# Twelve head-norm statistics, each as two single-pass matmuls on high and low parts, at later places in the matrix queue

## The reference

```python
    S_new, o = retention_scan(qf, kf, vf, ret_state.astype(jnp.float32))   # 4 heads, 256 values each
    o = o * lax.rsqrt(jnp.mean(o * o, axis=-1, keepdims=True) + EPS)       # the head norm
    o = o.reshape(B, T, RET_V_WIDTH).astype(xn.dtype)
    b_out = (jax.nn.silu(g) * o) @ w_ret_out
    merged = jax.nn.sigmoid(gate_a) * a_out + jax.nn.sigmoid(gate_b) * b_out
    return merged @ w_o, new_buf, S_new
```

## Time and profile before

| what | value |
|---|---|
| median of 3 runs (range) | 1497.55 us (1497.22 to 1497.59) |
| the profiled execution's span | 1495.6 us |
| outside the span, median less span | 1.95 us |
| PE busy | 1475.2 us (99%) |
| PE on the chain that ended last | 96% of the span |
| DVE, ACT, POOL busy | 1001.0, 635.4, 842.0 us |
| mean granted clock of PE | 0.997 |
| the 24 rows of L1194 (12 statistics) | 8.9 us of PE busy |

### The profile page before, as it was taken

The page is one execution under the profiler, slowest core; times in us unless marked ns, Lnnn a source line. Parts: engine busy times, 40 slices in busy tenths (PEclk is TensorE's granted clock), DMA queues, the critical chain, the costliest instruction groups (busy, mean ns, idle before and its releaser), DMA issues.

```text
span 1495.6 us, 28307 instructions
## 1 busy us (share of the span) xinstructions
PE 1475.2 (99%) x11336; PEld 1455.2 (97%) x11336; DVE 1001.0 (67%) x1251; ACT 635.4 (42%) x929; POOL 842.0 (56%) x571
## 2 busy tenths in 40 slices
PE   8999999999999999999999999999999999999996
PEld 5999999999999999999999999999999999999995
DVE  7999888856545724576715876766657765574847
ACT  5533444344544541131213855556556332332333
POOL 3377776777545653257565445555555655554555
PEclk9999999999999999999999999999999999999998
DMA  6013333322356258621421144566759575454634
GB/s 217 22 42 94 114 114 113 113 80 65 112 176 205 75 200 296 219 80 50 149 78 50 29 149 171 199 237 219 253 193 326 203 285 189 142 208 156 227 107 170
DMA packets 110091, 229.13 MB, mean 153 GB/s; under 512 B 8960, under 2 KB 20992, under 8 KB 108304
## 3 DMA queue, kind: packets, MB, share of 16 engines
q1 hardware_dynamic: 95296, 204.30, 39.7%
q10 hardware_dynamic: 14672, 23.09, 4.6%
HBM read 154.41 MB, written 72.95 MB: 152 GB/s over the span
## 4 chain that ended last, share of the span: by engine, by line
PE 96%; POOL 1%; DMA 1%; ACT 1%; issue 1%; DVE 0%; POOLq 0%; SPq 0%; DVEq 0%; ACTq 0%
PE ps L1476 40%; PE ps L1237 26%; PE ps L1026 16%; PE ps L1402 3%; PE ps L1389 3%; PE ps L1074 2%; PE ps L1164 1%; PE ps L1169 1%; PE ps L1180 1%; PE ps L1166 1%; DMA cva_h<-conv_scratch 1%; PE ps L1147 0%; PE ps L1152 0%; PE ps L1194 0%; POOL w_l L931 0%
## 5 line engine op out<-in xcount | busy, mean ns | idle before, releaser
L1476 PE MATMUL ps<-tx_h,w_h 128*128 128x258 f32 x960 | 271.5, 283 | 0.0
L1476 PE MATMUL ps<-tx_l,w_h 128*128 128x258 f32 x960 | 271.3, 283 | 0.0
L1476 PE MATMUL ps<-tx_h,w_l 128*128 128x258 f32 x960 | 271.1, 282 | 0.0
L996 POOL TENSOR_TENSOR w_l<-raw,w_h 128x512 fp32r<-128x512 f32 x120 | 185.6, 1551 | 147.6 <-ACT w_h L2033 147.1
L1476 PE MATMUL ps<-fx_l,w_h 128*128 128x258 f32 x720 | 203.7, 283 | 0.0
L1476 PE MATMUL ps<-fx_h,w_h 128*128 128x258 f32 x720 | 203.6, 283 | 0.0
L1476 PE MATMUL ps<-fx_h,w_l 128*128 128x258 f32 x720 | 203.4, 282 | 0.0
L1476 PEld LDWEIGHTS ps<-tx_h,w_h 128*128 128x128 f32 x960 | 181.4, 189 | 0.1
L1476 PEld LDWEIGHTS ps<-tx_l,w_h 128*128 128x128 f32 x960 | 181.4, 189 | 0.1
L1476 PEld LDWEIGHTS ps<-tx_h,w_l 128*128 128x128 f32 x960 | 181.2, 189 | 0.0
L2328 DVE SCALAR_TENSOR_TENSOR ps<-u_ext,wdw,ps 128x512 f32<-128x512 f32 x232 | 155.2, 749 | 0.0
(11 more groups left out here) (386 smaller groups left out, 4305.4 us busy)
## 6 DMA issues: line engine op xcount, KB each, us to landing
raw<-wseq_dram SPq DMA_DIRECT2D x260, 256.0 KB, 3.1
quad_scratch<-quad_h SPq DMA_DIRECT2D x16, 774.0 KB, 3.5
tx_h<-quad_scratch SPq DMA_DIRECT2D x12, 1032.0 KB, 10.4
tx_l<-hidden_scratch SPq DMA_DIRECT2D x12, 1032.0 KB, 12.8
gate_scratch<-gst SPq DMA_DIRECT2D x10, 1032.0 KB, 5.0
hidden_scratch<-hq_g SPq DMA_DIRECT2D x8, 1032.0 KB, 7.0
hidden_scratch<-stg_b SPq DMA_DIRECT2D x6, 1032.0 KB, 6.9
hq_g<-hidden_scratch SPq DMA_DIRECT2D x6, 1032.0 KB, 13.1
```

What stands on the lines that cost most here:

```text
L996: pool.tensor_tensor(lo, src, hi.bitcast(F32), ALU.subtract).then_inc(q_lo, 1)
L1476: out = pe.matmul(ps[:, 2 * n + s, 0:HC], RINGS[q % RING][wa][:, kk * P:(kk + 1) * P], OPS[x][xb][:, QK * kh + kk, at_:at_ + HC], start=(i ...
```

## The change

Each statistic is computed by two single-pass matmuls in place of one plain float32 matmul. To feed them, ACT copies the summed squares into a high part (`square_hi`), and DVE subtracts it to get the low part (`square_lo`). High and low parts have buffers of their own, so in the second pair a square no longer waits for the statistic two before it, but for that one's low part. The statistics stand later in PE's queue: one turn later in the first pair for i = 0, 1, 2, 4 and 5 and two for i = 3, and one or two slots later in the second. In the second pair squares, sums, roots and the decode store are reordered around them. Two semaphores are merged into others at the start of the kernel (`x0_sq` into `x_sq`, `hist_ld` into `wdw_ld`).

```diff
-NORM_SQUARE = {20: 0, 24: 1, 28: 2, 32: 3, 39: 4, 42: 5}
+NORM_SQUARE = {20: 0, 25: 1, 29: 2, 33: 3, 39: 4, 42: 5}
...
-NORM_STAT = {23: 0, 27: 1, 31: 2, 34: 3, 41: 4, 44: 5}
-NORM_SCALE = {26: 0, 29: 1, 33: 2, 35: 3, 42: 4, 45: 5}
...
+NORM_LO = {23: 0, 27: 1, 31: 2, 35: 3, 41: 4, 44: 5}
+NORM_STAT = {24: 0, 28: 1, 32: 2, 36: 3, 42: 4, 45: 5}
+NORM_SCALE = {26: 0, 30: 1, 33: 2, 37: 3, 43: 4, 46: 5}
...
+        osq_l = [place(f"osq_l{i}", [P, CH], F32R, (a_KT, a_Q, a_Q + 4 * CH)[i])[0] for i in range(3)]
+        osq_h = [place(f"osq_h{i}", [P, CH], F32R, (a_KT + 4 * CH, a_Q + 8 * CH, a_Q + 12 * CH)[i])[0]
+                 for i in range(3)]
...
             def out_stat(p, i):
-                pe.wait_ge(on_ad, 6 * p + i + 1)
+                pe.wait_ge(on_lo, 6 * p + i + 1)
...
-                pe.matmul(ps[:, 6 + i % 2, 0:CH], ones[:], osq[p * (i % 2)][:, 0:CH],
-                          start=True, stop=True).then_inc(on_st, 1)
+                k = p * (1 + i % 2)
+                pe.matmul(ps[:, 6 + i % 2, 0:CH], ones[:].bitcast(F32R), osq_h[k][:], start=True, stop=False)
+                pe.matmul(ps[:, 6 + i % 2, 0:CH], ones[:].bitcast(F32R), osq_l[k][:], start=False, stop=True
+                          ).then_inc(on_st, 1)
...
-            turns_ = {3: 0, 5: 1, 7: 2, 9: 3, 12: 4, 14: 5}
+            turns_ = {5: 0, 6: 1, 9: 2, 10: 3, 13: 4, 15: 5}
...
+            def square_hi(p, i):
+                k = p * (i % 2)
+                act.wait_ge(on_ad, 6 * p + i + 1)
+                act.activation(osq_h[p + k][:], osq[k][:, 0:CH], ACT.Copy).then_inc(on_hi, 1)
...
             norm_square(1, 1)
+            square_hi(1, 0)
+            square_hi(1, 1)
+            norm_square(1, 2)
             for i in range(2 * CHUNKS):
                 norm_root(1, i)
-                if i == 0:
+                if i + 2 < 2 * CHUNKS:
+                    square_hi(1, i + 2)
+                if i == 1:
                     decode_store(1, DEC - 1)
-                if i + 2 < 2 * CHUNKS:
-                    norm_square(1, i + 2)
+                if i + 3 < 2 * CHUNKS:
+                    norm_square(1, i + 3)
...
+            def square_lo(p, i):
+                k = p * (i % 2)
+                dve.wait_ge(on_hi, 6 * p + i + 1)
+                dve.tensor_tensor(osq_l[p + k][:], osq[k][:, 0:CH], osq_h[p + k][:].bitcast(F32), ALU.subtract
+                                  ).then_inc(on_lo, 1)
```

More of the change, by code:

```diff
@@ L100 @@
 SILU_ST = {4: 0, 10: 1, 14: 2, 19: 3}
-NORM_SQUARE = {20: 0, 24: 1, 28: 2, 32: 3, 39: 4, 42: 5}
-NORM_SUM = {21: 0, 26: 1, 30: 2, 33: 3, 40: 4, 43: 5}
-NORM_STAT = {23: 0, 27: 1, 31: 2, 34: 3, 41: 4, 44: 5}
-NORM_SCALE = {26: 0, 29: 1, 33: 2, 35: 3, 42: 4, 45: 5}
+NORM_SQUARE = {20: 0, 25: 1, 29: 2, 33: 3, 39: 4, 42: 5}
+NORM_SUM = {21: 0, 26: 1, 30: 2, 34: 3, 40: 4, 43: 5}
+NORM_LO = {23: 0, 27: 1, 31: 2, 35: 3, 41: 4, 44: 5}
+NORM_STAT = {24: 0, 28: 1, 32: 2, 36: 3, 42: 4, 45: 5}
+NORM_SCALE = {26: 0, 30: 1, 33: 2, 37: 3, 43: 4, 46: 5}
 ROPE = {(10, 0): ("mult", 0, 0, 0), (10, 2): ("mult", 0, 0, 1), (10, 3): ("join", 0, 0, 0),
@@ L271, in build @@
         x2_ld = sem("x2_ld")
-        x0_sq = sem("x0_sq")
         u_mm = sem("u_mm")
@@ L277, in build @@
         wdw_ld = sem("wdw_ld")
-        hist_ld = sem("hist_ld")
         piece_ld = [sem(f"piece_ld{i}") for i in range(4)]
@@ L349, in build @@
         on_ad = sem("on_ad")
+        on_hi = sem("on_hi")
+        on_lo = sem("on_lo")
         on_st = sem("on_st")
@@ L611, in _ @@
             sp.dma_start(x_in[:, :, 2 * CH:T], xT[:, :, 2 * CH:T]).then_inc(x2_ld, 16)
-            sp.dma_start(hist[:], cacheT).then_inc(hist_ld, 16)
+            sp.dma_start(hist[:], cacheT).then_inc(wdw_ld, 16)
             for n in range(2 * RAW, 16):
@@ L1595, in _ @@
             for i in range(4):
-                x_square(0, 2 * i, 2 * i + 2, xa_in[i], x0_sq)
+                x_square(0, 2 * i, 2 * i + 2, xa_in[i], x_sq)
             x_square(1, 0, 4, xb_in[0], x_sq)
@@ L1744, in norm_square @@
                     act.wait_ge(rp_st, 32)
-                if 6 * p + i:
-                    act.wait_ge(on_st, 6 * p + (i if p == 0 else max(i - 1, 0)))
+                if p and i > 1:
+                    act.wait_ge(on_lo, 6 + i - 1)
+                elif 6 * p + i:
+                    act.wait_ge(on_st, 6 * p + (i if p == 0 else 0))
                 if i == 4:
@@ L1801, in unit_turn @@
                     act.preload_act_table_set("natural_log_exp_and_others")
+                if x in NORM_SUM:
+                    square_hi(0, NORM_SUM[x])
                 if x in NORM_STAT:
@@ L2244, in square_half @@
                 if c:
-                    dve.wait_ge(x_sq, 2 * c + half - 1)
+                    dve.wait_ge(x_sq, 2 * c + half + 3)
                 else:
-                    dve.wait_ge(x0_sq, 2 * half + 2)
+                    dve.wait_ge(x_sq, 2 * half + 2)
                 return dve.tensor_tensor(q[:, a:a + 2], q[:, a:a + 2], q[:, a + 2:a + 4], ALU.add)
@@ L2343, in taps @@
                     n -= took
-            dve.wait_ge(wdw_ld, 48)
-            dve.wait_ge(hist_ld, 16)
+            dve.wait_ge(wdw_ld, 64)
             def u_out(j):
@@ L2566, in unit_turn @@
                     square_sum(0, NORM_SUM[x])
+                if x in NORM_LO:
+                    square_lo(0, NORM_LO[x])
                 if (v, j) in ROPE:
@@ L2642, in _ @@
             square_sum(1, 1)
+            square_lo(1, 0)
+            square_lo(1, 1)
+            square_sum(1, 2)
             head_norm(1, 0)
             decode_state(1, DEC - 1)
-            square_sum(1, 2)
-            product_gate(0)
+            square_lo(1, 2)
             head_norm(1, 1)
             square_sum(1, 3)
+            product_gate(0)
+            square_lo(1, 3)
+            product_gate(1)
             head_norm(1, 2)
-            product_gate(1)
             square_sum(1, 4)
+            square_lo(1, 4)
             head_norm(1, 3)
@@ L2654, in _ @@
             head_norm(1, 4)
+            square_lo(1, 5)
             product_gate(2)
```

## The result

| | before | after |
|---|---|---|
| median us (range), 10 runs each | 1497.48 (1497.15 to 1497.59) | 1500.95 (1499.67 to 1501.52) |
| span of the profiled execution | 1495.6 | 1499.2 |
| mean granted clock in it | 0.997 | 0.995 |

The ratio is 1.0022, with an interval of 1.0014 to 1.0030: 3.5 us slower. The forecast was 1499.3. The measured time lies within the range of 8 in 10 (1495.2 to 1501.5), but 0.15 us above the likeliest case's own range, and the change is twice the one forecast (+3.5 where +1.7 was expected). The single runs of after also spread over 1.9 us, those of before over 0.4.

A forecast was written before the change was run, and what follows sets the result against it. PE was taken as the bound, busy 99% of the span. Terms -3.2 + 0.7 + 2.5 + 1.7 = +1.7 us on the span 1495.6, plus 1.95 to the median, gave 1499.3 us; range of 8 in 10: 1495.2 to 1501.5.

The forecast's parts named there:

- the likeliest case: The forecast itself over the whole kernel: 1499.3 us, own range 1498.0 to 1500.8, chance 0.56.
- What PE saves: 12 x 0.27: PE's queue, both pairs: each statistic falls from 0.58 to 0.31 us, saving 3.2 us, 1.6 in each pair.
- First pair, unit 18: 0.7 lost: ACT's root of statistic 3 before the table loads lengthens PE's wait from 0.34 to about 1.0 us.
- Group 2: 0.25 + 2.25 us of waits: Second pair: PE waits 0.25 us for the decode state, then 2.25 for DVE's product gate; together 2.5, bounds 1.9 to 3.5.
- Groups 4 and 5: 1.7, between 0.4 and 2.9: Second pair behind group 2: later statistics and DVE's queue delay group 5, 1.7 us more lost.
- a hold of sum 4: Second pair, DVE: sum 4 held behind POOL's second addition makes group 5 3.8 us late; one hold in about half the cases.
- Held steps: Second pair: DVE's low parts or sums may be blocked behind POOL; 1.5 us late without holds, 3.8 with every low part exposed.
- rival 1: Second pair: DVE's low part or sum is held behind POOL in each pass; 1500.5 to 1501.6 us, chance 0.23.
- rival 4: Both pairs: the matmul pair is no cheaper than float32, leaving the waits alone; 1502.4 us, chance 0.03.
- Rivals 2 to 4: Only ACT's table place costs, 1495.0 (0.14); all saving stands, 1494.1 (0.04); pair no cheaper than float32, 1502.4 (0.03).
- The merged semaphores at no cost: Merged semaphores wait for the same instructions at the same places: no cost.
- Behind group 5 nothing gives time back: After group 5, PE is on the chain to the end, so no lost time is recovered.

The follow-up runs named there:

- e4: Changed kernel with one plain float32 matmul on the high part in place of each single-pass pair, low part computed but not added: 1501.85 us, ratio 1.0033.
- e5: e1 with ACT's root of statistic 3 behind unit 18's table loads and DVE's decode copy ahead of the rope multiplications: 1497.01 us, ratio 0.9999.
- e9: e5 with statistic 3's whole chain one turn earlier, its root in ACT's gap ahead of the table loads: 1496.51 us, ratio 0.9992.
- e2: Changed kernel with DVE's last decode state ahead of head norm 0 and group 0's product gate directly behind it: 1499.78 us, ratio 1.0016.
- e10: e2 without POOL's additions for groups 0 and 1, their semaphore still raised: 1496.54 us, ratio 0.9993.
- e3: Changed kernel with 12 extra single-pass matmuls, results unused, on PE ahead of group 2: 1502.21 us, ratio 1.0029.
- e1: Changed kernel with the second pair put back as before, so the first pair's part alone: 1497.63 us, ratio 1.0001.
- e6: e1 with four chained extra additions of 344 columns on DVE ahead of group 0's product gate: 1499.26 us, ratio 1.0014.
- e8: Changed kernel with the first pair put back to float32 at the old turns, so the second pair's part alone: 1500.62 us, ratio 1.0024.
- e11: All twelve pairs: e9's first pair, e2's DVE order in the second, POOL's additions for groups 0 and 1 moved later: 1496.47 us, ratio 0.9992.
- e12: e11 with group 2's product gate ahead of head norm 4 in DVE's order: 1495.63 us, ratio 0.9986.
- e7: e1 with six chained extra additions of 344 columns on DVE ahead of group 1's product gate: 1500.41 us, ratio 1.0021.

## Why the prediction was right, and where it was not

- *What PE saves: 12 x 0.27.* Right: 0.33 or less a pair, and e4 brought back 0.58.
- *First pair, unit 18: 0.7 lost.* Right in size (0.8 against 0.2 in the list of waits), and the root stood where it was said. e5 and e9 confirm the cause: what counts is ACT's full stretch, and only a place outside it helps. Missed: 0.4 us for a decode copy behind DVE's multiplication of 1.78 us. The multiplication was as long before (1.79), but statistic 0 stood at this place in PE's queue and covered the wait (477.15 to 477.74); it now stands one product later. By these rows the pair gains 0.6, and its turns gain 0.5 in the trace, not 0.9. That the stage began 0.86 us sooner, near my 0.9, is luck: 0.4 of it is the load of `cva_h`.
- *Group 2: 0.25 + 2.25 us of waits.* Right in place, releaser and order; measured 0.22 + 1.79. DVE's row was 0.3 us shorter than my sum, since its steps overlap in their starts (low part 0.42 and sum 0.43 in the chain, where I took 0.5), and the decode product added 1.05 us behind its wait and not 0.79.
- *Groups 4 and 5: 1.7, between 0.4 and 2.9.* This is the step that failed. It began "From 652.35 two slots, statistic 2, a slot ...", with each slot at the full-clock rate of the earlier trace rows: the clock behind a new wait was put at full without a word. In the trace, the two slots and the statistic behind the wait took 6.12 us and not 3.24. The term came out at 3.8, 2.9 of it by the clock; without the fall it would have been 0.9, so the rest was rated too high. The prediction also gave a hold of sum 4 one chance in two. In the profiled run sum 4 was free (0.51 us); sum 5 was held by 0.35 us, by a weight split and not by an addition, and the wait for group 4 was 0.56.
- *Held steps.* The earlier trace rows had one such row; e2's two (1.97 and 1.45 us) and e10, in which they took 0.82 and 0.51 without the additions, show the same: each held sum ended 0.4 us behind the addition. POOL's weight splits hold too, which the prediction did not count: in after the low parts 0 and 1 took 1.36 and 1.60 us and sum 5 0.86, each ending 0.4 us behind a split. The rule is that of the Trainium skill (SBUF — State Buffer, on the shared port pair): a VectorE instruction with two SBUF inputs and a GpSimd instruction that reads SBUF exclude each other for a whole instruction. The trace agrees: sums and low parts have both inputs in SBUF, and the held ones end just behind POOL's instruction.
- *The time.* That 1500.95 still lies inside the range of 8 in 10 is in part luck. The range reached so high for rival 1's holds and rival 4's dearer pairs; a lower clock was in none of its cases, and without the fall the traces' sum would be +0.7 (3.6 less 2.9) with all else as it was, below the forecast's +1.7. But e3 shows that all else would not have been as it was: PE, arriving sooner, met a held sum.
- *Rivals.* Rival 1 (held low parts decide, 1500.5 to 1501.6) gives the right time for a reason that is not the main one in the changed kernel; it decides in e2 and e3. Rivals 2 to 4 are out: there were 2.6 us of waits, and the pair is cheaper.
- *The merged semaphores at no cost.* Held as far as the traces go. All twelve experiments keep them, and at the decode product at 470 us (470.35 before) six of them are 0.01 to 0.11 us early and five 0.03 to 0.17 late. Only e1 and after are 0.4 late.
- *Behind group 5 nothing gives time back.* Held: 3.8 us late there (0.4 - 0.86 + 4.26), 3.6 at the end.

Open: what decides in which execution the clock falls, and whether after's spread of 1.9 us is this alone. The wait for `sgt` at 38 us (1.0 us in after and e1, 0.3 to 0.7 in e3, e6, e8, e9, e11 and e12, none in before, e2, e4, e5, e7 and e10) and the load of `cva_h` (late in e1 and e11, a little in before) follow no edit of mine. The kernel before's two separate semaphores were not tried with the rest, so that the merge has to do with the wait for `sgt` is not excluded.

## What to carry to other kernels

A cheaper instruction on the busiest engine pays only as far as the chains that feed it are not the next limit: list, for each moved step, what its feeders' queues do between its release and its use, and reorder those queues in the same change (e12: -1.8 us, where the bare change gave +3.5). Price a new wait of the matrix engine at its length and, as a second case, with a lower clock behind it (here 1.7 to 2.9 us more, behind waits of 1.6 to 2.2). Where a new DVE step reads two SBUF tiles, look for POOL's long instructions beside it, and move these first.

## What the runs showed of the hardware that was not expected

- Behind a wait of 1.79 us on PE, and ahead of that eight one-column matmuls and 0.22 us of wait, the granted clock was 0.50 for 5.8 us (1.2 GHz level). Behind 1.64 us it was 0.66 over 5 us, behind 2.20 us 0.72 over 6 us, and behind 1.61 us in e2's profiled run it stayed at 1.00. The float32 statistic took 1.15 us at the lower level and 0.58 at the full one.
- Two single-pass matmuls of 344 columns took 0.31 to 0.33 us where one float32 matmul took 0.58.
- An addition of 344 columns on DVE took 0.51 us alone and up to 2.51 beside an addition of 1032 columns on POOL, which it then outlasted by 0.4 us. A subtraction of the same width took 0.51 us alone and 1.36 and 1.60 beside weight splits of 512 columns.
